# Half-turned tiles 6 and 7 behind a normed phase of a one-core decoder trunk

## The reference, cut to what matters

```python
def rms_norm(x, g):
    ms = jnp.mean(x * x, axis=-1, keepdims=True)
    return x * lax.rsqrt(ms + EPS) * g

h = h + rms_norm(mix, post_mix_g[layer])        # mix: output of a projection
f = conv_ffn(rms_norm(h, pre_ffn_g[layer]), ...)  # first step: rms_norm(h) @ w_up
h = h + rms_norm(f, post_ffn_g[layer])
```

## Time and profile before

| what | value |
|---|---|
| median of 3 runs | 2141.93 us (2141.06 to 2142.15) |
| the profiled execution's own time | 2140.77 us |
| its span, first to last instruction | 2139.0 us |
| mean granted clock of PE | 0.999 |
| PE, DVE, ACT, POOL busy | 2129.6, 1432.1, 1014.8, 72.7 us |
| seams with half-turned tiles | 3, starting at 282.33, 1014.73 and 1399.96 us |

### The profile page before, as it was taken

One profiled execution on the slowest core, in us unless ns is written; L12 is line 12 of the kernel. 1 busy time (PEld: TensorE's weight loads), 2 busy tenths in 40 slices (PEclk: granted clock), 3 DMA queues, 4 the chain that ended last, 5 costly groups with the idle time before them and its releaser, 6 DMA issues.

```text
span 2139.0 us, 32149 instructions
## 1 busy us (share of the span) xinstructions
PE 2129.6 (100%) x11273; PEld 1826.9 (85%) x11273; DVE 1432.1 (67%) x1758; ACT 1014.8 (47%) x1174; POOL 72.7 (3%) x99
## 2 busy tenths in 40 slices
PE   9999999999999999999999999999999999999998
PEld 8888888888888888888888888888888888888887
DVE  5666577777877774444765675577878778774444
ACT  6445464444444444434644574464444444444433
POOL 0510010000000000000000010010000000000000
PEclk9999999999999999999999999999999999999999
DMA  7865656666666566665566544656666666666664
GB/s 258 231 207 176 198 175 190 187 184 196 188 193 187 177 218 199 193 193 180 187 189 189 177 154 154 204 175 189 189 180 198 189 193 187 180 221 192 193 195 149
DMA packets 210686, 407.31 MB, mean 190 GB/s; under 512 B 13488, under 2 KB 15920, under 8 KB 209968
## 3 DMA queue, kind: packets, MB, share of 16 engines
q1 hardware_dynamic: 207920, 398.51, 60.8%
q0 software_dynamic: 2640, 7.73, 1.1%
q10 hardware_dynamic: 48, 0.02, 0.0%
HBM read 404.10 MB, written 2.10 MB: 190 GB/s over the span
## 4 chain that ended last, share of the span: by engine, by line
PE 99%; issue 0%; ACT 0%; DVE 0%; DVEq 0%; POOLq 0%; POOL 0%; ACTq 0%
PE ps L1440 37%; PE ps L1443 18%; PE ps L1456 13%; PE ps L1454 13%; PE ps L1455 13%; PE ps L1407 1%; PE ps L1410 1%; PE ps L1371 1%; PE ps L1533 1%; PE ps L1374 0%; PE ps L1550 0%; PE ps L1612 0%; PE ps L1680 0%; PE ps L1651 0%; PE ps L1512 0%
## 5 line engine op out<-in xcount | busy, mean ns | idle before, releaser
L887 DVE TENSOR_TENSOR w_lo<-raw,w_hi 128x1024 fp32r<-128x1024 f32 x743 | 905.7, 1225 | 633.6 <-ACT w_hi L539 628.3
L539 ACT CAST w_hi<-raw 128x1024 fp32r<-128x1024 f32 x749 | 781.3, 1050 | 930.3 <-PE ps L1443 526.9
L1440 PE MATMUL ps<-x_parts,w_hi 128*128 128x512 f32 x3136 | 1089.3, 394 | 0.0
L1443 PE MATMUL ps<-x_parts,w_lo 128*128 128x256 f32 x3136 | 869.7, 277 | 0.0
L1440 PEld LDWEIGHTS ps<-x_parts,w_hi 128*128 128x128 f32 x3136 | 588.1, 188 | 137.2
L1443 PEld LDWEIGHTS ps<-x_parts,w_lo 128*128 128x128 f32 x3136 | 589.1, 188 | 0.0
L1454 PE MATMUL ps<-w_hi,g_parts 128*128 128x512 f32 x704 | 274.1, 389 | 0.0
L1456 PE MATMUL ps<-w_hi,g_parts 128*128 128x512 f32 x704 | 273.9, 389 | 0.0
L1455 PE MATMUL ps<-w_lo,g_parts 128*128 128x512 f32 x704 | 273.9, 389 | 0.0
L1455 PEld LDWEIGHTS ps<-w_lo,g_parts 128*128 128x128 f32 x704 | 132.1, 188 | 27.4
L1456 PEld LDWEIGHTS ps<-w_hi,g_parts 128*128 128x128 f32 x704 | 132.1, 188 | 27.4
(11 more groups left out here) (163 smaller groups left out, 1740.8 us busy)
## 6 DMA issues: line engine op xcount, KB each, us to landing
raw<-in_ffn_w_up SPq DMA_DIRECT2D x352, 512.0 KB, 3.7
raw<-in_ffn_w_down SPq DMA_DIRECT2D x176, 512.0 KB, 4.5
raw<-in_a_w_in SPq DMA_DIRECT2D x61, 512.0 KB, 4.6
raw<-in_a_w_out SPq DMA_DIRECT2D x32, 512.0 KB, 4.7
raw<-in_b_w_q SPq DMA_DIRECT2D x32, 512.0 KB, 4.5
raw<-in_w_k SPq DMA_DIRECT2D x32, 512.0 KB, 4.6
raw<-in_w_v SPq DMA_DIRECT2D x32, 512.0 KB, 4.7
raw<-in_b_w_o SPq DMA_DIRECT2D x32, 512.0 KB, 4.6
```

Source lines behind the costliest of these rows:

```text
L539: act.copy(w_hi[:, slot, :, :], raw[:, slot, :, :]).then_inc(unit_hi, 1)
L887: dve.tensor_tensor(w_lo[:, slot, :, :], raw[:, slot, :, :], w_hi[:, slot, :, :].bitcast(F32), ALU.subtract).then_inc(unit_split, 1)
L1440: pe.matmul(ps[:, bank + m, :], w_hi[:, slot, kk, m * P:(m + 1) * P], src[:, kt, :, :].rearrange("p a t -> p (a t)"), start=first, stop=False,
L1443: mm = pe.matmul(ps[:, bank + m, 0:T], w_lo[:, slot, kk, m * P:(m + 1) * P], src[:, kt, HI, :], start=False, stop=last, skip_group_check=True)
```

## The change

It makes `EARLY` four, and splits what `EARLY` meant: slots 0 to 3 are half 0 of tiles 0 to 7, slots 4 to 7 half 1 of tiles 0 to 7, slots 8 to 11 tiles 8 to 15 whole, while only the first `APART = 3` units are multiplied in halves. Slot 3 (half 0 of tiles 6 and 7) is turned just ahead of slot 4, whose data the update of half 1 gives. The last slots are turned behind unit 4, not 3. The high part of unit 2 is now a copy on DVE (`third_high`) and its low part is DVE's too; POOL makes only the low part of unit 1, behind the first update of half 1. ACT and DVE get new written orders. The numbers of matmuls and transposes stay what they were (32 transposes at a seam, three units in halves).

```diff
@@ slots @@
-        EARLY = 3
+        EARLY = 4
+        APART = 3
-        SLOT_BANK = [4, 5, 6, 4, 5, 6, 7, 4, 5, 6, 7]
-        SLOT_BEFORE = {3: 0, 4: 1, 5: 2, 7: 3, 8: 4, 9: 5, 10: 6}
+        SLOT_BANK = [4, 5, 6, 4, 5, 6, 7, 4, 5, 6, 7, 4]
+        SLOT_BEFORE = {3: 0, 4: 1, 5: 2, 7: 3, 8: 4, 9: 5, 10: 6, 11: 7}
@@ POOL, for each normed phase s @@
                 for half in range(NH):
                     rsqrt(post_scale[:, half:half + 1], post_mean[:, half:half + 1], 1,
                           post_meaned, post_scaled, NH * s + half + 1)
-                    if s + 1 < len(NORMED):
-                        if half:
-                            pool.wait_ge(h_new[1], NB * s + 2)
-                        unit_low(BEHIND[s], half + 1)
                 if s + 1 < len(NORMED):
+                    pool.wait_ge(h_new[1], NB * s + 1)
+                    unit_low(BEHIND[s], 1)
                     pre_rsqrt(s + 1)
@@ ACT, turn_and_split @@
-                slot_keep(t, (1,))
-                units(ph.first, 2, 3)
-                slot_high(t, (3, 4))
-                slot_keep(t, (2,))
-                units(ph.first, 3, RING)
-                slot_keep(t, (3,))
-                slot_high(t, (5, 6))
-                slot_keep(t, (4,))
+                act.wait_ge(unit_hi, ph.first + 3)
+                if t != KV_NORM:
+                    units(ph.first, 3, RING)
+                act.wait_ge(evacuated, ph.block0)
+                slot_high(t, (3,))
+                if t == KV_NORM:
+                    units(ph.first, 3, RING)
+                slot_high(t, (4, 5))
+                slot_keep(t, (3, 4))
+                slot_high(t, (6, 7))
+                slot_keep(t, (5,))
                 units(ph.first, RING, RING + 1)
-                slot_keep(t, (5,))
-                slot_high(t, (7, 8))
+                slot_keep(t, (6,))
+                slot_high(t, (8, 9))
+                slot_keep(t, (7,))
+                square_stream(t, 0)
                 units(ph.first, RING + 1, RING + 2)
-                square_stream(t, 0)
-                slot_high(t, (9, 10))
+                slot_high(t, (10, 11))
                 units(ph.first, RING + 2, RING + 3)
@@ ACT, after_normed @@
-                slot_keep(s + 1, (0,))
+                slot_keep(s + 1, (0, 1, 2))
@@ DVE, new, called in after_normed behind update_stream(s, 1, 0) @@
+            def third_high(ph):
+                dve.wait_ge(raw_loaded[2], 16 * (ph.first // RING + 1))
+                dve.wait_ge(unit_used, ph.first + 2 - RING + 1)
+                dve.wait_ge(unit_hi, ph.first + 2)
+                dve.tensor_copy(w_hi[:, 2, :, :], raw[:, 2, :, :]).then_inc(unit_hi, 1)
@@ DVE, turn_and_split @@
+                gain_block(t - 1, LAST, (1,))
                 update_first(t - 1)
+                slot_low(t, (3, 4))
                 update_stream(t - 1, 1, 1)
-                slot_low(t, (3,))
-                gain_block(t - 1, LAST, (1,))
-                slot_low(t, (4,))
+                slot_low(t, (5,))
+                dve.wait_ge(unit_split, ph.first + 2)
+                units(ph.first, 2, 3)
                 update_stream(t - 1, 2, 0)
                 update_stream(t - 1, 2, 1)
-                slot_low(t, (5, 6))
-                slot_keep(t, (6,))
-                dve.wait_ge(unit_split, ph.first + EARLY)
+                slot_low(t, (6, 7))
                 units(ph.first, 3, RING)
+                slot_low(t, (8, 9))
+                units(ph.first, RING, RING + 1)
                 update_stream(t - 1, 3, 0)
                 update_stream(t - 1, 3, 1)
-                slot_low(t, (7,))
-                units(ph.first, RING, RING + 1)
-                slot_low(t, (8,))
-                slot_keep(t, (7, 8))
+                slot_keep(t, (8, 9))
                 units(ph.first, RING + 1, RING + 2)
-                slot_low(t, (9,))
-                units(ph.first, RING + 2, RING + 3)
-                slot_low(t, (10,))
-                units(ph.first, RING + 3, ph.units)
-                slot_keep(t, (9, 10))
+                slot_low(t, (10, 11))
+                units(ph.first, RING + 2, ph.units)
+                slot_keep(t, (10, 11))
@@ PE, first_columns @@
-                for u in range(EARLY):
-                    if u == EARLY - 1:
-                        turn_slots(t, (3, 4))
+                for u in range(APART):
+                    if u == APART - 1:
+                        turn_slots(t, (3, 4, 5))
...
                     if u == 0:
-                        turn_slots(t, (5,))
                         pe.wait_ge(evacuated, ph.block0)
-                        turn_slots(t, (6,))
+                        turn_slots(t, (6, 7))
                     if u == 1:
-                        turn_slots(t, (7, 8))
-                for u in range(EARLY, ph.units):
+                        turn_slots(t, (8, 9))
+                for u in range(APART, ph.units):
...
                     if u == EARLY:
-                        turn_slots(t, (9, 10))
+                        turn_slots(t, (10, 11))
```

More of the change, by code:

```diff
@@ L1192, in after_normed @@
                 update_stream(s, 1, 0)
+                third_high(nxt)
                 slot_low(s + 1, (0, 1, 2))
@@ L1405, in first_columns @@
                             if m == 0:
-                                pe.wait_ge(x_ready, x_whole(t, kt))
+                                pe.wait_ge(x_ready, x_tile(t, EARLY + u, kk) if u < EARLY else x_whole(t, kt))
                             pe.matmul(ps[:, bank + m, :], w_hi[:, slot, kk, m * P:(m + 1) * P],
```

## The result

The changed kernel takes 2154.92 us in the median of 17 runs, the kernel before 2141.03 (17 runs, 2140.32 to 2142.15): slower by 13.9 us (by the means a ratio of 1.0060, 95% interval 1.0049 to 1.0072). I had forecast +4.5 us, 2146.4 with a range up to 2148.4. So the direction was right and the size wrong: by 9.4 us in the difference, and by 8.5 in the time, because the median of the kernel before is now 0.9 lower than the 2141.93 that I added to.

The account below looks back on a forecast made before the run. PE was taken as the bound, busy 2129.6 of 2139.0 us. Seam terms of +1.4, +1.8 and +1.4 us, less a tenth, gave +4.5 on 2141.93: 2146.4 us, range 2144.2 to 2148.4.

Parts of the forecast that it names:

- Part 5: Last transposes one unit later: PE waits 0.95 us for the split of unit 6, at all three seams.
- Parts 1 and 4: Slot 3's transposes inside the stall, -0.2 us a seam; wait ahead of slot 8, +0.56 us, first and third seams.
- Parts 2 and 3: DVE's `third_high` copy, 0.70 us, and `gain_block` ahead of `update_first`, in DVE's wait for POOL: both cost 0.
- Part 4: POOL's later subtraction holds DVE's update until 2.22 us after POOL's start; PE waits 0.56 us, first and third seams.
- Part 6: Unit 8's split ready about when PE arrives: 0.1 us of wait a seam, all slack used up.
- Part 7: Second seam: unit 3's cast between highs of slots 3 and 4 makes PE wait 0.95 us, hiding the slot 8 wait.
- The sum: First and third seams +1.4 us each, second +1.8, together 4.6, less a tenth: +4.5 us.
- D: Rival: further waits downstream, ACT's order delaying units 8 or 9 by 0.3 to 0.6 us a seam; +5.9 us, chance 0.10.

Follow-up runs that it names:

- Experiment 2: Changed kernel, with ACT casting and DVE splitting unit 6 ahead of the last two slots' highs and lows: six runs, 2143.17 to 2163.24 us.
- kernel 7: Kernel before, with two idle ACT copies ahead of unit 8's cast so that its split ends around PE's arrival: six runs, 2149.72 to 2162.33 us.
- kernel 12: Changed kernel, ACT's squares and unit 6's cast and split ahead of the last slots, unit 3's cast first at the second seam: 2141.48 to 2163.19 us.
- kernels 8 and 9: Changed kernel, last turns back behind unit 3: median 2142.38 us; the second also casts unit 3 first at the second seam: 2141.88 us.

## Why the prediction was wrong

**The start was wrong in one sentence.** "So only two things can change the time: the work of PE ... and the moments at which PE stands still." There is a third, the pace at which PE runs the same work; the prediction had no term for it. The trace of before held it: at the first seam the pairs of unit 3 lie 0.353 us apart, and those of units 4 and 5 behind the last transposes, which begin in the rows at 297.33, 0.347. More plainly, `gate_u` runs slow there and `up0` quick. In the view of engine use of the kernel before, with the columns as above, a stretch of each:

```profile
100.00:150.00 50.00, 50.00 (x285) 43.33 (x284) 37.07 (x38) 22.55 (x22) 8.64 (x5) 1.00 0.66 203
400.00:450.00 50.00, 50.00 (x290) 43.74 (x289) 40.31 (x54) 22.55 (x22) 0.00 (x0) 1.00 0.64 190
```

The run-to-run spread of the kernel before, under 2 us, gave no warning, since its order happens to come out the same way each time. 2145.64, the median of the five runs that by their time have no slow phase, is what the parts sum to; the other 9.3 us of the median are pace.

**Part 5, the largest, was right in what it worked out and missed what mattered.** The wait ahead of unit 6 cost 0.9 us at each seam for 0.95. (Experiment 2 against the change gives 0.90, 1.01 and 1.00; in the last two 0.1 us is already the slow pace, of the 16 pairs from the wait to the spread.) But moving the last transposes behind a second unit costs more by the draw of the pace than by the wait, and I looked only for who waits.

**Parts 1 and 4.** With unit 6's wait removed, the first and third seams are 26.5 us against 26.18: +0.33, my -0.2 + 0.56 = +0.36. The two terms by starts: PE begins half 1 of unit 1 0.19 us earlier, and the wait ahead of slot 8 is 0.45 us for 0.56. The remaining 0.05 us are pace again: unit 4 now stands ahead of the last transposes, with 8 more slow pairs.

**Parts 2 and 3** held: 0.69 us for 0.70, and the gain inside the gap.

**Part 4's mechanism** held: POOL starts 0.08 behind the update's end, and the update of chunk 1 is held until 288.67 - 0.75 = 287.92, which is 2.19 us behind POOL's start (for 2.22). The rule of the page "SBUF — State Buffer" of the Trainium skill, section "Who interferes with whom", is that a DVE instruction with two SBUF inputs and a GpSimd instruction that reads SBUF lock each other out; the rows agree. The update came 1.33 us behind POOL's start here and 1.76 before, and was let go at the same point, which fits an exclusion better than a slowing down.

**Part 6.** I put 0.1 us of wait at unit 8. It is 0.02 at most (a step of 333 ns for 313 at seam 1), and in the changed kernel's profile no seam changed its pace there. But that the split comes just in time can by itself draw the pace, as kernel 7 shows. "The change has used up all slack" was the right remark with the wrong price.

**Part 7** was right in kind: by starts PE waits 1.0 us at the second seam for 0.95 (0.9 in the list), and this hides the wait of part 4 (kernel 12).

**The sum** of the seams measured 1.23 + 1.86 + 1.31 = 4.4 us for 4.5. A little of that agreement is luck: the wait of part 4 was put 0.1 us too high at two seams, and 0.05 to 0.15 us of slow pairs at each seam was not in the sum. Of the rivals, D looked at the right place for kernel 7, unit 8, but priced a wait there, at +5.9 us in all against +13.9; none had the mechanism.

What stays open: why 8 or 16 slow pairs make the difference. 16 and 8 leave different rests in a pattern of three pairs, but I ran no third number. Which part of PE holds the pattern was not tried. Nor did I find a way to keep `gate_u`, slow in every profile here, at the quick pace, which would give 256 x 0.0067 = 1.7 us.

## What to carry to other kernels

A change that costs 4 us by its waits can cost 14 by what it does to a long stream of identical matmuls behind them; so count matmuls per 100 us in untouched stretches of both traces before explaining anything at the place of the change. If single runs of a kernel fall in steps, divide the step by the number of repeated instructions in a phase. And look at the margin between the last producer and PE ahead of such a stream. The kernel before and kernels 8 and 9, which are steady, have 0.77 us at unit 8; kernel 7, with the same order of PE and a split that PE met with a wait of 0.06 us, is spread. Where between the two the trouble begins was not measured.

## What the runs showed of the hardware

PE's pace for alternating matmuls of 512 and 256 columns with new weights each has two values at the same granted clock of 1.00, 347 and 353 ns a pair. It was kept for up to 475 us, in every profiled phase to its end. It was drawn anew where the stream was broken by transposes or by a wait, the shortest of them 0.06 us (kernel 7). The quick pace has two forms (231, 112, 233, 117 ns and 230, 117 ns) that both last 346.7 ns a pair over a phase, but react differently to the next two transposes. The phases of 512-column matmuls alone (226.7 ns from start to start) showed nothing of the kind in any of the fourteen profiles.
